# Four column tiles of 32 rows for eight of sixteen experts, and three experts fixed in advance, in a one-core inference step

## The chip, the core and the metric

The kernel runs on one core of a Trainium2 chip. The core has a matmul engine (TensorE, PE in the rows; PEld is its weight load), VectorE (DVE), ScalarE (ACT), GpSimd (POOL) and SyncE (SP), which here only issues DMAs. Sixteen DMA engines move data between the chip's memory (HBM), SBUF and DRAM scratch tensors. The metric is the device time of one execution in microseconds. Everything is fp32.

## The reference

One layer of a hybrid backbone on 128 context tokens and 256 latent tokens of width 1024. The part before the experts (norm, modulation, a state-space mixer, a gated MLP mixer, the output projection) is not touched by the change. The part that is:

```python
scores = sigmoid(h @ router_w); sel = scores + router_b          # 16 experts in 4 groups
g = argmax over groups of the sum of the group's top 2 of sel
expert = top 2 of sel within group g;  w = scores[expert] / sum
hg = h @ w_gate[e];  hu = h @ w_up[e]                            # 1024 -> 512
moe = sum over the two experts of w * ((silu(hg) * hu) @ w_down[e])   # 512 -> 1024
x = x + gate2 * moe;   y = rmsnorm(x, final_norm_w)
```

384 tokens choose two experts each: 768 pairs. With the inputs drawn by setup_inputs the experts 0 to 15 get 108, 37, 143, 90, 9, 41, 48, 32, 16, 18, 12, 4, 63, 52, 18 and 77 pairs. An expert's weights are 2 MiB of gate, 2 MiB of up and 2 MiB of down, so the sixteen are 96 MiB, and each is read once.

## The kernel before

**Stages.** Up to about 240 us of the span the mixers and the output projection run. Then the router picks the experts (240 to 258 us), and the tokens are sorted by expert: GpSimd scatters every token's row to a scratch tensor in HBM, `sorted_tokens` (`hsd`), at the place of its pair, and six tiles of 128 rows are read back (`hsr`, one `hs_in` semaphore each), transposed on TensorE (`sorted_columns`, L738) and copied by ACT and DVE into `hTs`. While that goes on, TensorE already works on the first expert, whose rows it picks by one-hot matmuls (L825, L832).

**Places.** The experts are worked on in sixteen places. Place 0 is expert 0 and place 1 expert 1, so that their weights load long before the router has run; the others are ordered on the chip by their number of pairs, by a key of ranks (`turn_key`). Pairs of one place lie side by side in `sorted_tokens`.

**Passes.** A pass takes 64 rows of one place. `gate_up` (L754) holds 64 rows as stationary operand in two column tiles and streams 512 columns (256 of gate and 256 of up) through each; 8 chunks of the contraction times 2 tiles is 16 matmuls. An fp32 matmul here leaves two records in the trace, so a pass shows 32. `down` (L767) is 8 matmuls, 16 records. Between them ACT takes silu of the gate half out of PSUM (`gate`, L1110), DVE multiplies (`multiply`, L1661), TensorE transposes the product (`transposes`, L777, 2 records) and DVE copies it back (`turn_over`, L1666). The order on TensorE is a pipeline: gate_up of the next pass, then down of the pass before, then the transposes of the next. ACT copies the result of down (`evacuate`, L1125) and sends it with two DMAs to `sorted_outputs` (L1129); before it sends, it waits until the pass before has landed. A place with more than 64 rows has a second pass, with more than 128 a third. What is left of the possible passes is made up for by adding to the semaphores (`skipped`), which count PASSES per place on every engine.

**Weights.** Three sets of buffers. Place p uses set p % 3, and SP loads it in `reload`: gate and up (four DMAs, L389) when all gate_up passes of place p-3 are done, down (one DMA, L394) when the last down of place p-3 is done, which on TensorE comes after the first gate_up of place p-2. SP's DMAs are in program order.

**The start.** The sets of places 0 and 1 load from 180 us on. Set 2 is known only after the router: its buffers overlap those of the sorted tiles, so SP loads the gate weights after `int_done` (the integers that the engines branch on) and the up and down weights after the last sorted tile is transposed (`hs_ready` 12, L430). Then comes place 3.

**The end.** The last three passes stay in SBUF; the other results are picked up by GpSimd from `sorted_outputs` (L1916), and TensorE adds all up (L863, L886). Then the final norm and the output.

The names that the change and the prediction touch: `load_gate_up`, `load_down`, `reload` (SP), `gate_up`, `down`, `transposes`, `skipped`, `second_pass`, `sorted_columns` (PE), `gate`, `evacuate`, `last_pass`, `sorted_copy` (ACT), `stage_x` (L1656, which copies the rows of a place into the stationary buffer `xs`), `turn_over`, `multiply`, `to_next` (DVE).

## Time and profile before

| what | us |
|---|---|
| median of three runs | 545.04 (544.37 to 546.21) |
| span of the profiled execution, first to last instruction | 544.1 |
| PE busy in the span | 480.4 (88%) |
| DVE, ACT, POOL busy | 236.0, 148.2, 104.4 |
| moved by DMA | 164.64 MB, mean 303 GB/s |

The profile gives the profiled execution as its span alone; what lies around it is in the runs' own times, whose median is 0.9 us above that span. Busy time of PE counts pipelined matmuls with modelled ends, so a busy PE is not one at its peak. The span in 40 slices of 13.6 us shows three parts: until slice 17 the mixers, slices 18 and 19 the router with no DMA at all, then from slice 22 on the experts, with PE at nine tenths or more and the DMA engines full at the same time, and at the end three slices in which the DMA is nearly empty. A DMA share slightly above 1 is a full one.

### The profile page before, as it was taken

What the parts mean: (1) busy time and instruction counts of PE and PEld (TensorE: products, weight loads), DVE (VectorE), ACT (ScalarE), POOL (GpSimd) and SP (SyncE); (2) the same over time, 40 slices, a digit from 0 to 9 for tenths busy, and PEclk for the clock granted to TensorE, in tenths of its full rate; (3) what the DMA queues carried; (4) which work ended last, traced back from release to release, by engine and by line L of the source; (5) the groups of instructions that cost most, each with busy time, mean ns of one, the idle gap of its engine ahead of it and who ended that gap; (6) DMA issues with size and microseconds to landing.
All of it is one profiled execution on the core that took longest, in us unless ns stands there. A gap on an engine that the chain in (4) does not pass through costs nothing. (4 is left out here: it accounts for less than half of the span.)

```text
span 544.1 us, 8978 instructions
## 1 busy us (share of the span) xinstructions
PE 480.4 (88%) x3278; PEld 233.3 (43%) x3279; DVE 236.0 (43%) x590; ACT 148.2 (27%) x289; POOL 104.4 (19%) x187
## 2 busy tenths in 40 slices
PE   2788979899969999995996999899998999999893
PEld 1135669655559644573344333333333333333331
DVE  2698994999963300867663101111011101111045
ACT  3645794532147610151102010110001100101142
POOL 3000250988870203500500000000000000000300
PEclk9988999999999999995998999999999999999998
DMA  8993046449497999220696999999999999999932
GB/s 278 339 400 112 1 154 217 166 166 363 143 391 269 369 366 417 82 86 1 239 385 243 410 423 418 418 418 416 421 421 419 419 417 419 417 420 421 403 120 116
DMA packets 42571, 164.64 MB, mean 303 GB/s; under 512 B 3314, under 2 KB 4106, under 8 KB 32676
## 3 DMA queue, kind: packets, MB, share of 16 engines
q1 hardware_dynamic: 35440, 144.22, 67.3%
q10 hardware_dynamic: 4580, 11.91, 5.8%
q0 software_dynamic: 2512, 7.99, 4.0%
q8 instruction: 24, 0.39, 0.3%
q14 instruction: 15, 0.12, 0.1%
HBM read 152.77 MB, written 11.34 MB: 302 GB/s over the span
## 5 line engine op out<-in xcount | busy, mean ns | idle before, releaser
L754 PE MATMUL psum<-arena 128*64 128x512 f32 x672 | 150.7, 601 | 16.7 <-DVE arena L1656 7.8
L754 PEld LDWEIGHTS psum<-arena 128*64 128x64 f32 x672 | 49.8, 138 | 103.7 <-issue 101.9
L767 PE MATMUL psum<-arena 128*64 128x512 f32 x336 | 75.9, 592 | 0.0
L1661 DVE TENSOR_TENSOR arena<-arena,psum 128x256 f32<-128x256 f32 x21 | 8.8, 421 | 143.4 <-ACT arena L1110 143.2
L1916 POOL DMA_INDIRECT arena<-sorted_outputs,src_u x6 | 5.7, 951 | 244.1 <-DMA sorted_outputs<-arena 242.6
L767 PEld LDWEIGHTS psum<-arena 128*64 128x64 f32 x336 | 25.7, 137 | 45.9 <-issue 45.9
L1110 ACT ACTIVATE arena<-psum 128x256 f32<-128x256 f32 x21 | 8.0, 383 | 130.0 <-PE psum L754 114.5
L664 PE MATMUL psum<-arena 128*128 128x512 f32 x96 | 42.2, 594 | 0.0
L1125 ACT ACTIVATE arena<-psum 128x512 f32<-128x512 f32 x19 | 11.3, 597 | 58.0 <-PE psum L767 58.0
L664 PEld LDWEIGHTS psum<-arena 128*128 128x128 f32 x96 | 17.9, 190 | 21.2 <-issue 20.9
L1656 DVE COPY arena<-arena 128x512 f32 x31 | 13.1, 423 | 30.4 <-issue 30.4
L487 PE MATMUL psum<-arena 128*2 128x512 f32 x64 | 18.4, 734 | 8.1 <-DMA arena<-in_w_mod 8.1
L528 PE MATMUL psum<-arena 128*128 128x388 f32 x64 | 23.8, 521 | 1.1 <-ACT arena L957 1.1
L940 ACT ACTIVATE arena<-arena 128x512 f32<-128x512 f32 x32 | 20.9, 715 | 7.7 <-DVE arena L1371 7.7
L536 PE MATMUL psum<-arena 128*128 128x388 f32 x64 | 21.1, 491 | 0.0
L617 PE MATMUL psum<-arena 128*128 128x512 f32 x48 | 20.9, 594 | 0.0
L1666 DVE COPY arena<-psum 128x256 f32<-128x256 f32 x21 | 8.9, 425 | 25.3 <-PEq L786 13.7
L1860 POOL TENSOR_TENSOR arena<-arena 128x64 f32<-128x64 f32 x32 | 14.8, 464 | 22.3 <-DVEq L1462 19.9
L472 PE MATMUL psum<-arena 128*2 128x128 f32 x512 | 15.4, 273 | 1.4 <-DMA arena<-in_w_mod 1.4
L528 PEld LDWEIGHTS psum<-arena 128*128 128x128 f32 x64 | 12.4, 203 | 9.0 <-issue 3.0
L1862 POOL TENSOR_TENSOR arena<-arena 128x64 f32<-128x64 f32 x32 | 15.2, 476 | 2.5
L536 PEld LDWEIGHTS psum<-arena 128*128 128x128 f32 x64 | 12.1, 190 | 8.4
(355 smaller groups left out, 657.3 us busy)
## 6 DMA issues: line engine op xcount, KB each, us to landing
arena<-in_w_gate SPq DMA_DIRECT2D x32, 1024.0 KB, 15.7
arena<-in_w_up SPq DMA_DIRECT2D x32, 1024.0 KB, 18.1
arena<-in_w_down SPq DMA_DIRECT2D x16, 2048.0 KB, 15.2
arena<-in_w_mod SPq DMA_DIRECT2D x12, 2048.0 KB, 13.0
arena<-in_w_in SPq DMA_DIRECT2D x3, 2048.0 KB, 19.2
sorted_outputs<-arena ACTq DMA_DIRECT2D x38, 128.0 KB, 6.3
arena<-in_w_out SPq DMA_DIRECT2D x2, 2048.0 KB, 16.7
arena<-modulation_rows ACTq DMA_DIRECT2D x4, 1024.0 KB, 10.7
```

Source lines behind the costliest of these rows:

```text
L472: last = mm(out[t], sil[:, k, :], w[:, k, t * P:t * P + P], start=(k == 0), stop=False)
L487: last = mm(bank[(4, 7)[c]][32 * t:32 * t + 2, :], sil[:, k, :], w[:, kk, t * D + c * 512:t * D + c * 512 + 512], start=(k == 0), stop=(k ...
L528: last = mm(bank[c][:, 0:TOK], w[:, k, c * P:(c + 1) * P], h1T[:, k, :], start=(k == 0), stop=(k == KD - 1))
L536: last = mm(out, w[:, k, c * P:(c + 1) * P], h1T[:, k, :], start=(k == 0), stop=(k == KD - 1))
L617: last = mm(bank[b][:, :], h1T[:, k, T0[t]:T0[t] + P], w[:, k, :], start=(k == 0), stop=(k == KD - 1))
L664: last = mm(bank[OUT_BANK[2 * t + h]][:, :], yT[:, k, T0[t]:T0[t] + P], wout[h][:, k, :], start=(k == 4), stop=(k == 3))
L754: last = mm(bank[0][HALF * t:HALF * t + HALF, :], xs[:, side, k, :], gu[:, :, k, t * 256:t * 256 + 256], start=(k == 0), stop=(k == KD - 1))
L767: last = mm(bank[4][HALF * h:HALF * h + HALF, :], hiddenT[:, s * P + t * HALF:s * P + t * HALF + HALF], dn[:, 2 * t + s, h * 512:h * 512 + ...
L940: last = A(out[:, :, 16 * g:16 * g + 16], made[i % 4], ACT.Copy, scale=side[:, c:c + 1])
L1656: cp(xs[:, side], hTs[:, :, bass.ds(row, HALF)]).then_inc(S("x_staged"), 1)
L1860: p(G.tensor_tensor(pt1, prev, Tre, ALU.mult))
L1862: w(G.tensor_tensor(nxt, nxt, pt1, ALU.add))
```

## The change

1. **Lots of 32.** Places 1, 2, 4, 5, 7, 8, 10 and 11 (`in_parts`) run in passes of 32 rows. `gate_up` then uses four column tiles of 32 stationary columns and streams 256 columns through each: 32 matmuls a pass, 64 records. `down` is 16 matmuls of 256 columns. There is one transpose in place of two, and ACT, DVE and the two DMAs of a result handle half as much. PASSES is 12 in place of 6; the loop over places handles its three places by name (one full, two in parts), and the last three places are written out.
2. **Three fixed experts.** Places 0, 1, 2 are the experts 0, 4 and 8 (EARLY), with 108, 9 and 16 pairs. The other thirteen are ordered by a new key. With the pairs above the places hold:

| place | 0 | 1 | 2 | 3 | 4 | 5 | 6 | 7 | 8 | 9 | 10 | 11 | 12 | 13 | 14 | 15 |
|---|---|---|---|---|---|---|---|---|---|---|---|---|---|---|---|---|
| pairs before | 108 | 37 | 90 | 63 | 52 | 48 | 41 | 143 | 32 | 18 | 77 | 18 | 16 | 12 | 9 | 4 |
| passes of 64 before | 2 | 1 | 2 | 1 | 1 | 1 | 1 | 3 | 1 | 1 | 2 | 1 | 1 | 1 | 1 | 1 |
| pairs now | 108 | 9 | 16 | 143 | 37 | 32 | 90 | 18 | 18 | 77 | 12 | 4 | 63 | 52 | 48 | 41 |
| passes of 64 now | 2 | - | - | 3 | - | - | 2 | - | - | 2 | - | - | 1 | 1 | 1 | 1 |
| passes of 32 now | - | 1 | 1 | - | 2 | 1 | - | 1 | 1 | - | 1 | 1 | - | - | - | - |

3. **Loads.** The buffers change places: the third set's gate and up lie where the output projection's weights were, and load when that projection's last matmul is done (`wo_ready` 6). The sorted tiles lie over the third set's down buffer (`h2`'s slot); tiles 0, 1, 2 and 4 load as before, tile 3 after `int_done`, and tile 5 takes tile 0's place, so ACT issues its load after tile 0 is transposed. SP issues the gate and up weights of place 3 when the second gate_up of place 0 is done, ahead of the wait for the sorted tiles; the down weights of place 2 after that wait, and those of place 3 after the last down of place 0. TensorE's code for place 0 is written out so that the semaphore `gated` is topped up right after the second gate_up.
4. Some small operations on DVE (the number of passes for lots of 32) ahead of `int_done`, and four on POOL (`in_parts`).

```diff
-PASSES = 6
+PASSES = 12
+FULL = 6
+PART = 32
+EARLY = (0, 4, 8)
-        hsr = view(slot(7), 6, D)
+        hsr = [view(at, D) for at in (slot(6), slot(6) + 1024, slot(6) + 2048, slot(6) + 3072, F + 12544, slot(6))]
-            b = (3, 0, 6)[j]
-            return view(slot(b), 2, KD, DE), view(slot(b + 2), 4, D)
+            gu, dn = ((3, 5), (0, 2), (7, 6))[j]
+            return view(slot(gu), 2, KD, DE), view(slot(dn), 4, D)
...
             sp.wait_ge(S("fin_done"), 1)
-            load_gate_up(0, 0)
-            load_down(0, 0)
+            load_gate_up(0, EARLY[0])
+            load_down(0, EARLY[0])
             sp.wait_ge(S("unit_used"), 15)
-            load_gate_up(1, 1)
+            load_gate_up(1, EARLY[1])
             sp.wait_ge(S("yt_done"), 4)
             sp.wait_ge(S("modd_in5"), 32)
-            load_down(1, 1)
+            load_down(1, EARLY[1])
+            sp.wait_ge(S("wo_ready"), 6)
+            load_gate_up(2, EARLY[2])
+            def load_sorted(t):
+                sp.dma_start(hsr[t], hsd[t * P:(t + 1) * P, :]).then_inc(S(f"hs_in{t}"), 16)
             sp.wait_ge(S("tok_sent"), 16 * 6)
-            for t in range(6):
-                sp.dma_start(hsr[:, t, :], hsd[t * P:(t + 1) * P, :]).then_inc(S(f"hs_in{t}"), 16)
-            sp.wait_ge(S("first_ready"), 1)
+            sp.wait_ge(S("pad_sent"), 48)
+            sp.wait_ge(S("first_ready"), 4)
+            for t in (0, 1, 2):
+                load_sorted(t)
+            load_sorted(4)
             sp.wait_ge(S("onehots_done"), 1)
-            sp.wait_ge(S("pad_sent"), 48)
             sp.wait_ge(S("int_done"), 1)
-            third = expert_at(2)
-            for k, sem in ((0, "gu_in2"), (KD // 2, "gu_rest2")):
-                sp.dma_start(expert_weights(2)[0][:, 0:1, k:k + KD // 2],
-                             wg[:, bass.ds(third, 1), k:k + KD // 2, :]).then_inc(S(sem), 16)
+            load_sorted(3)
+            fourth = expert_at(SETS)
+            sp.wait_ge(S("gated"), PASSES)
+            load_gate_up(0, fourth)
             sp.wait_ge(S("hs_ready"), 12)
...
-            def gate_up(j, at, fresh, side=0):
+            def gate_up(j, at, fresh, side=0, part=False):
+                rows, cols = (PART, P) if part else (HALF, 256)
...
                 for k in range(KD):
-                    for t in range(2):
-                        last = mm(bank[0][HALF * t:HALF * t + HALF, :], xs[:, side, k, :],
-                                  gu[:, :, k, t * 256:t * 256 + 256], start=(k == 0), stop=(k == KD - 1))
+                    for t in range(P // rows):
+                        last = mm(bank[0][rows * t:rows * t + rows, 0:2 * cols], xs[:, side, k, 0:rows],
+                                  gu[:, :, k, t * cols:t * cols + cols], start=(k == 0), stop=(k == KD - 1))
                 last.then_inc(S("gated"), 1)
-            def down(j, fresh, turned, evacuated):
+            def down(j, fresh, turned, evacuated, part=False):
-                for s in range(2):
-                    for t in range(2):
-                        for h in range(2):
-                            last = mm(bank[4][HALF * h:HALF * h + HALF, :],
-                                      hiddenT[:, s * P + t * HALF:s * P + t * HALF + HALF],
-                                      dn[:, 2 * t + s, h * 512:h * 512 + 512],
-                                      start=(s == 0 and t == 0), stop=(s == 1 and t == 1))
+                if part:
+                    for t in range(4):
+                        for h in range(4):
+                            last = mm(bank[4][PART * h:PART * h + PART, 0:256], hiddenT[:, t * PART:t * PART + PART],
+                                      dn[:, t, h * 256:h * 256 + 256], start=(t == 0), stop=(t == 3))
+                else:
+                    for s in range(2):
+                        for t in range(2):
+                            for h in range(2):
+                                last = mm(bank[4][HALF * h:HALF * h + HALF, :],
+                                          hiddenT[:, s * P + t * HALF:s * P + t * HALF + HALF],
+                                          dn[:, 2 * t + s, h * 512:h * 512 + 512],
+                                          start=(s == 0 and t == 0), stop=(s == 1 and t == 1))
                 last.then_inc(S("downed"), 1)
-            def transposes(at):
+            def transposes(at, part=False):
                 pe.wait_ge(S("multiplied"), at + 1)
-                for s in range(2):
+                for s in range(1 if part else 2):
...
+            def part_rest(j, e, use):
+                n = pe.value_load(n_i[0:1, bass.ds(e, 1)], min_val=0, max_val=NT * P)
+                def part_pass(at):
+                    gate_up(j, at, None, 0, True)
+                    down(j, use + 1, at, at + -1, True)
+                    transposes(at, True)
+                with pe.If(n > PART):
+                    gate_up(j, turn(1, e), None, 1, True)
+                    down(j, use + 1, turn(1, e), turn(0, e), True)
+                    transposes(turn(1, e), True)
+                    with pe.If(n > HALF):
+                        with pe.Fori(2, 6) as q:
+                            part_pass(q + turn(0, e))
...
-                later_passes(0, 0, 0, first_n)
+                gate_up(0, turn(1, 0), None, 1)
+                with pe.If(first_n > P):
...
+                with pe.Else():
+                    pe.wait_ge(S("gated"), turn(2, 0))
+                    pe.sem_inc(S("gated"), PASSES - 2)
+                    down(0, 1, turn(1, 0), turn(0, 0))
+                    transposes(turn(1, 0))
+                    pe.wait_ge(S("crossed"), turn(2, 0))
+                    pe.wait_ge(S("downed"), turn(2, 0))
+                    pe.sem_inc(S("crossed"), PASSES - 2)
+                    pe.sem_inc(S("downed"), PASSES - 2)
+                    sorted_tiles()
...
-                    expert_rest((j + 1) % SETS, e + 1, use)
+                    use, other = i + (j + 1) // SETS, (j + 1) % SETS
+                    gate_up(other, turn(0, e + 1), use + 1, 0, other > 0)
+                    down(j, i + 1, turn(PASSES, e), turn(PASSES - 1, e), j > 0)
+                    transposes(turn(0, e + 1), other > 0)
+                    if other > 0:
+                        part_rest(other, e + 1, use)
+                    else:
+                        expert_rest(other, e + 1, use)
+            for j in range(SETS):
...
-            def evacuate(y, downed, before, row):
+            def evacuate(y, downed, before, row, part=False):
                 act.wait_ge(S("downed"), downed + 1)
-                A(ystage[:, y, :], bank[4][:, :], ACT.Copy).then_inc(S("evacuated"), 1)
+                cols = 256 if part else 512
+                A(ystage[:, y, 0:cols], bank[4][:, 0:cols], ACT.Copy).then_inc(S("evacuated"), 1)
                 act.wait_ge(S("evacuated"), before + 2)
                 act.wait_ge(S("written"), before * 32 + 32)
                 for h in range(2):
-                    act.dma_start(ysd[bass.ds(row, HALF), h * 512:h * 512 + 512],
-                                  ystage[HALF * h:HALF * h + HALF, y, :]).then_inc(S("written"), 16)
+                    half = ystage[HALF * h:HALF * h + HALF, y, 0:cols]
+                    if part:
+                        dst = ysd[bass.ds(row, PART), h * 512:h * 512 + 512].rearrange("r (q c) -> q r c", q=2)
+                    else:
+                        dst = ysd[bass.ds(row, HALF), h * 512:h * 512 + 512]
+                    act.dma_start(dst, half).then_inc(S("written"), 16)
...
-            for t in range(6):
+                second_pass(0, 2)
+            sorted_copy(0)
+            act.wait_ge(S("hs_ready"), 2)
+            act.dma_start(hsr[5], hsd[5 * P:6 * P, :]).then_inc(S("hs_in5"), 16)
+            for t in range(1, 6):
...
+            rank, turn_key, counted_rank = r1[:, 0, :], key, r2[:, 0, :]
             v(V_.tensor_reduce(rank, larger, AX.X, ALU.add))
-            v(ts(turn_key, rank, 0.15, None, ALU.mult))
-            for r in (2.0, 4.0):
-                v(stt(turn_key, rank, r, turn_key, ALU.is_equal, ALU.add))
+            v(ts(counted_rank, rank, 0.5, 1.75, ALU.mult, ALU.add))
+            v(stt(counted_rank, rank, 9.5, counted_rank, ALU.is_lt, ALU.mult))
+            v(stt(turn_key, rank, 0.5, counted_rank, ALU.mult, ALU.add))
```

DVE has the same three changes as ACT: a `part` argument that halves the columns of `multiply` and `turn_over` and the rows of `stage_x`, a `part_rest`, and the loop over three places.

SP's instructions from the load of place 1's down weights to the gate weights of place 3 (sorted_tokens are the sorted tiles, 128x2048 a half of a gate or up matrix), before:

```order
L394 DMA arena<-in_w_down 128x4x1024 [waits modd_in5,yt_done]
L419 DMA arena<-sorted_tokens 128x1024 [waits tok_sent]
L419 DMA arena<-sorted_tokens 128x1024 x5
L398 TENSOR_LOAD exp_i [waits pad_sent,int_done,onehots_done,first_ready]
L398 ISA x2
L426 ISA
L426 DMA arena<-in_w_gate 128x2048
L426 ISA
L426 DMA arena<-in_w_gate 128x2048
L430 DMA arena<-in_w_up 128x2048 [waits hs_ready]
L430 DMA arena<-in_w_up 128x2048
L394 DMA arena<-in_w_down 128x4x1024
```

and now:

```order
L393 DMA arena<-in_w_gate 128x2048 [waits wo_ready]
L393 DMA arena<-in_w_up 128x2048
L393 DMA arena<-in_w_gate 128x2048
L393 DMA arena<-in_w_up 128x2048
L425 DMA arena<-sorted_tokens 128x1024 [waits first_ready,pad_sent,tok_sent]
L425 DMA arena<-sorted_tokens 128x1024 x3
L425 DMA arena<-sorted_tokens 128x1024 [waits int_done,onehots_done]
L402 TENSOR_LOAD exp_i
L402 ISA x2
L393 ISA [waits gated]
L393 DMA arena<-in_w_gate 128x2048
L393 DMA arena<-in_w_up 128x2048
```

The four loads of place 2 have moved ahead of the sorted tiles, one sorted tile is gone from the queue and another has a wait of its own, and the loads of place 3 now wait for TensorE's gate_up alone. Behind them stand the two loads of down weights, of place 2 and of place 3, and then the loads of place 4:

```order
L398 DMA arena<-in_w_down 128x4x1024 [waits hs_ready]
L398 DMA arena<-in_w_down 128x4x1024 [waits downed]
L402 TENSOR_LOAD exp_i
L402 ISA x2
L393 ISA [waits gated]
```

Before, only `hs_ready` stood between the sorted tiles and the loads of places 2 and 3, now a load of down weights stands on each of two waits.

ACT's queue at the sorted tiles (L1129 or L1218 sends place 0's first result, L1114 or L1197 copies a sorted tile out of PSUM), before:

```order
L1129 DMA sorted_outputs<-arena 64x512
L1129 ISA
L1129 DMA sorted_outputs<-arena 64x512
L1175 UNCONDITIONAL_BRANCH
L1114 ACTIVATE arena<-psum 128x4x128 [waits hs_ready] x6
```

and now:

```order
L1218 DMA sorted_outputs<-arena 64x512
L1218 ISA
L1218 DMA sorted_outputs<-arena 64x512
L1288 UNCONDITIONAL_BRANCH
L1197 ACTIVATE arena<-psum 128x4x128 [waits hs_ready]
L1292 DMA arena<-sorted_tokens 128x1024 [waits hs_ready]
L1197 ACTIVATE arena<-psum 128x4x128 [waits hs_ready] x5
```

The load of tile 5 stands behind the two result DMAs and the copy of tile 0, and TensorE's last eight transposes wait for it.

## Rows read from the trace of the kernel before

**Rows 1.** DMA between 300 and 480 us: packets and rate, queues, landing times.

```profile
DMA packets 14932, 75.34 MB, mean 419 GB/s; under 512 B 1385, under 2 KB 1385, under 8 KB 9137
q1 hardware_dynamic: 12525, 71.31, 96.0%
sorted_outputs<-arena ACTq DMA_DIRECT2D x32, 128.0 KB, 6.4
```

**Rows 2.** Stretches: PE, PEld, DVE, ACT, POOL busy us, PE clock, DMA share, GB/s.

```profile
236.00:260.00 24.00, 17.69 (x87) 12.00 (x87) 17.08 (x62) 8.25 (x15) 1.06 (x1) 0.64 0.00 1
...
288.00:292.00 4.00, 1.96 (x18) 1.77 (x16) 2.08 (x4) 1.55 (x3) 0.00 (x0) 1.00 0.28 55
292.00:296.00 4.00, 2.42 (x8) 0.77 (x10) 1.09 (x3) 0.00 (x0) 0.00 (x0) 0.73 1.00 403
296.00:300.00 4.00, 4.00 (x18) 1.33 (x16) 0.00 (x0) 0.00 (x0) 0.00 (x0) 0.84 0.98 395
```

**Rows 3.** Timeline of PE: start, duration, instructions [idle before, releaser]; places 0 to 2.

```profile
272.71 7.09 PE L754 MATMUL psum<-arena 128*64 128x512 f32 x32 [0.67 <-issue]
279.62 3.61 PE L767 MATMUL psum<-arena 128*64 128x512 f32 x16
...
286.15 3.81 PE L738 MATMUL psum<-arena 128*128 128x128 f32 x32 [0.77 <-ACT arena L1114]
293.58 8.78 PE L754 MATMUL psum<-arena 128*64 128x512 f32 x32 [3.62 <-DVE arena L1656]
302.19 3.61 PE L767 MATMUL psum<-arena 128*64 128x512 f32 x16
305.73 0.44 PE L777 MATMUL psum<-arena 128*128 128x128 f32 x2
306.88 7.09 PE L754 MATMUL psum<-arena 128*64 128x512 f32 x32 [0.72 <-PEq L786]
...
317.70 7.09 PE L754 MATMUL psum<-arena 128*64 128x512 f32 x32
```

**Rows 4.** Timeline of PE, the place with three passes and the next.

```profile
376.49 7.09 PE L754 MATMUL psum<-arena 128*64 128x512 f32 x32 [1.03 <-DVE arena L1656]
...
409.91 7.09 PE L754 MATMUL psum<-arena 128*64 128x512 f32 x32 [0.89 <-PEq L786]
...
421.49 7.09 PE L754 MATMUL psum<-arena 128*64 128x512 f32 x32 [0.69 <-PEq L786]
```

**Rows 5.** Timeline of PE where four column tiles are used.

```profile
80.45 1.93 PE L472 MATMUL psum<-arena 128*2 128x128 f32 x64
82.20 0.40 PE L476 MATMUL psum<-arena 128*2 128x128 f32 x8
...
93.43 0.87 PE L581 MATMUL psum<-arena 128*32 128x96 f32 x32
94.11 0.48 PE L587 MATMUL psum<-arena 128*32 128x32 f32 x32
```

**Rows 6.** Timeline of SP, the waiting loads.

```profile
289.99 0.81 SPq L430 DMA_DIRECT2D arena<-in_w_up  x2
...
305.83 0.39 SPq L394 DMA_DIRECT2D arena<-in_w_down  x1
...
409.24 0.33 SPq L389 DMA_DIRECT2D arena<-in_w_gate  x1
```

**Rows 7.** Timelines: DVE and ACT at place 0, DVE at place 1.

```profile
271.12 0.42 DVE L1661 TENSOR_TENSOR arena<-arena,psum 128x256 f32<-128x256 f32 x1 [2.07 <-ACT arena L1110]
...
284.04 1.32 ACTq L1129 DMA_DIRECT2D sorted_outputs<-arena  x2
...
305.35 0.43 DVE L1656 COPY arena<-arena 128x512 f32 x1 [2.11 <-issue]
```

**Rows 8.** DMAs that write or read sorted_tokens, shortest, median and longest.

```profile
DMA to landing us min/median/max: 3.2/5.1/8.4
```

**Rows 9.** Timeline of PE at the last place.

```profile
507.10 3.65 PE L754 MATMUL psum<-arena 128*64 128x512 f32 x16 [0.83 <-DMA arena<-in_w_up]
```

More of the change, by code:

```diff
@@ L216, in build @@
         fin = small(2, Q)
+        in_parts = small(NE)
         epsc = small(1)
@@ L850, in _ @@
             with pe.Else():
                 skipped(0, 1)
-            with pe.Fori(0, 5) as i:
+                sorted_tiles()
+            with pe.Fori(0, 4) as i:
                 for j in range(SETS):
                     e = i * SETS + j
-                    use = i + (j + 1) // SETS
-                    gate_up((j + 1) % SETS, turn(0, e + 1), use + 1)
-                    down(j, i + 1, turn(PASSES, e), turn(PASSES - 1, e))
-                    transposes(turn(0, e + 1))
-                    expert_rest((j + 1) % SETS, e + 1, use)
+                    use, other = i + (j + 1) // SETS, (j + 1) % SETS
[6 more added lines that the diff above has]
+                        expert_rest(other, e + 1, use)
@@ L861, in late_part @@
+            for j in range(SETS):
+                e = 4 * SETS + j
+                use, other = 4 + (j + 1) // SETS, (j + 1) % SETS
+                gate_up(other, turn(0, e + 1), use + 1)
+                down(j, 5, turn(PASSES, e), turn(PASSES - 1, e))
+                transposes(turn(0, e + 1))
+                expert_rest(other, e + 1, use)
             def late_part(part, t, h):
@@ L1105, in _, with gate @@
                       S("first_staged"), 1)
-            def gate(at):
+            def gate(at, part=False):
+                cols = P if part else 256
                 act.wait_ge(S("gated"), at + 1)
-                A(sg[:, :], bank[0][:, 0:256], ACT.Silu).then_inc(S("silued"), 1)
+                A(sg[:, 0:cols], bank[0][:, 0:cols], ACT.Silu).then_inc(S("silued"), 1)
             def sorted_copy(t):
@@ L1776, in _ @@
                 skipped(0, 1)
-            with dve.Fori(0, NE - 1) as e:
+            with dve.Fori(0, 4) as i:
+                for j in range(SETS):
+                    e, other = i * SETS + j, (j + 1) % SETS
+                    to_next(e, j > 0, other > 0)
+                    if other > 0:
+                        part_rest(e + 1)
+                    else:
+                        expert_rest(e + 1)
+            with dve.Fori(4 * SETS, NE - 1) as e:
                 to_next(e)
```

192 lines of the change are left out of this document (140 added, 52 removed).

## The prediction, made before the changed kernel was run

> **What bounds the kernel now.** I read the strip of 40 slices first, then stretches of a few us, then the timelines of PE and SP. From slice 22 on two resources are full together. The DMA engines move 419 GB/s without a gap from 300 to 480 us, 71.3 MB of it weights on SP's queue [rows 1]. PE starts a new place 11.6 to 11.8 us after the last and a further pass of the same place 10.8 us after the pass before: 306.88 to 317.70 in place 2, and 33.4 for the three passes from 376.49 to 409.91 [rows 3, 4]. Twenty passes from 293.58 on end at the last gate_up. Which of the two ends last is seen at the last place: the second half of its gate_up starts at 507.10 and was released by the DMA of up weights, after only 0.83 us of waiting [rows 9]. So both arrive together. After it comes a tail of down, adding up and the final norm that the change leaves alone: 544.1 - 507.1 = 37 us. The question is when the last gate and up weights land, T, now 507.
>
> The weight stream starts at 290.9: SP issued at 289.99 and the stretch 288 to 292 has a DMA share of 0.28, 1.1 us of 4 [rows 2, 6]. Before that lies a hole: from 236 to 260 the DMA is all but empty [rows 2].
>
> **PE's part of the change.** Now 13 passes are of 64 rows and 9 of 32. Four column tiles already run in this kernel: 64 records of 128 columns take 82.20 - 80.45 = 1.75 us, 27.3 ns each, and 32 records with 32 stationary columns and 96 streamed take 0.68 us, 21 ns each [rows 5]. Two tiles of 512 columns take 279.62 - 272.71 = 6.91 us for 32 records, 216 ns each [rows 3]. By columns 128 at 27.3 is 256 at 54.6, so gate_up of 32 rows is 64 x 54.6 = 3.5 us in place of 6.9, and down 32 x 54.6 = 1.75 in place of 3.54 (305.73 - 302.19). The row of 21 ns says that loading 32 columns ahead of each record fits under that. What follows a gate_up before the next place's rows are staged doesn't shrink: from the end of place 1's gate_up (302.19) to the end of DVE's copy (305.78) 3.6 us [rows 3, 7]. A place in one part thus takes 3.5 + 3.7 = 7.2 us, or 8.2 behind a full down, against 11.7. Summed by places 3 to 14: 33.4 + 14.5 + 7.2 + 22.6 + 8.2 + 7.2 + 22.6 + 8.2 + 7.2 + 3 x 11.7 = 166 us, while twelve places of weights take 12 x 6.29 MB / 0.40 = 189. PE falls out of the bound; the stream sets the end.
>
> **What the stream saves.** From its start to T it carries 80 MiB of weights before (up of place 2, its down, twelve places, gate and up of the last). Now gate and up of place 2 load at 237, in the hole, and gate and up of place 3 when the second gate_up of place 0 ends, at 279.8, when DMA has only sorted tiles left. 72 MiB stay: 8.4 MB less. The results written shrink as well, 64 KB a DMA for a part: 18 passes x 0.262 = 4.7 MB before, 10 x 0.262 + 9 x 0.131 = 3.8 MB now. Together 9.3 MB / 419 = 22.2 us less.
>
> **What it pays: a later start.** The down weights of place 2 wait for the last sorted tile, those of place 3 for the last down of place 0, and behind the latter waits everything else on SP's queue, in program order. Tile 5 is loaded only after tile 0 is transposed, on ACT's queue behind the two result DMAs, which end at 285.36 [rows 7]. With 0.6 for ACT's copy of tile 0 and 0.3 for TensorE's new wait on its own semaphore ahead of down, the issue is at 286.3. The landing is not in the trace. Bounds: 3.2 and 8.4, the ends of the row of DMAs of that tensor [rows 8]; the nearest row is a result DMA of ACT behind the weight stream, 6.4 [rows 1]. I take 6.5: 292.8. Its eight transposes take 3.81 / 4 = 0.95, so 293.8 against 289.96. From there to place 1's gate_up 3.6 as before: 297.4 against 293.58.
>
> That gate_up follows idle time. Before, after 3.6 idle us, the clock was 0.73 in 292 to 296 and 0.84 in 296 to 300, part of it at 1.2 GHz, and gate_up took 8.78 for 7.09, 1.7 lost [rows 2, 3]. Now PE idles longer, in two pieces, and the clock is likely at 1.2 GHz from the first record; I take 2.0 lost (bounds 0 and 3.5): end at 302.9. Down of place 0 ends 3.54 later, 306.4; SP issues 0.1 later (305.83 against 305.73) and data flow 0.9 after that: 307.4, where the stream before started at 290.9. Cost 16.5 us.
>
> **A stall at place 3.** Place 3 now holds 143 pairs, three full passes. Place 2's gate_up starts 4.7 after place 1's ended (302.19 to 306.88): 307.6, takes 3.5, and place 3's starts 3.7 later, 314.8. Gate and up of place 6 wait for all of place 3's passes: before, the three-pass place started at 376.49 and SP issued at 409.24, 32.75 later [rows 4, 6]. So 347.5, data at 348.4. Until then the queue holds down 3, gate, up and down of 4 and of 5: 14 MiB and 1.05 MB of results, 15.7 MB / 419 = 37.5 us from 307.4, which is 344.9. The stream stands still for 3.5 us. At place 6 (two passes, SP's issue 21.9 after its start) the same sum gives 393 against a queue that lasts to 396, and at place 9 still more room: no stall.
>
> Sum: -22.2 + 16.5 + 3.5 = -2.2 us. The last gate_up starts after idle time too, up to 1.7 lost, most of it under the wait between its halves: +0.2. The small DVE operations (six of 0.2 us ahead of `int_done`) add up to 1.2 and are hidden under gate_up of place 0, for which DVE idles 2.07 us before its product [rows 7]. The sum is made on the span of 544.1; the runs' median is 0.9 above it, and I carry the difference of -2.0 over: **543.0 us**.
>
> **Two rules from the skill.** The row has ACT's DMAs of 128 KB land in 6.4 us behind a full SP queue [rows 1]. The Trainium skill (DMA: Bandwidth & Descriptors, Queues, rings and completion order) says that each DMA engine takes the queues in turn, packet by packet. By that tile 5, four times as large, would share with place 3's weights and land in some 6.4 + 0.39 MB / 210 = 8.3 us, for a sum of -0.4 instead of -2.2; only part of it counts, as those weights end near 291.
>
> PE lost 1.7 us after 3.6 idle us [rows 2, 3]. The Trainium skill (TensorE: Matmul & The Clock Gate, HAM oscillation) warns that a kernel which waits for DMA between bursts of matmuls goes back to half clock at each of them. That speaks against making PE the engine that waits, and is rival 3.
>
> **Rivals.**
> 1. *The start is less late.* Tile 5 lands in 3.2 us, because place 3's weights are nearly through: place 1 starts at 294.1, with a clock loss as before. -2.0 - 3.3 - 0.3: 539.4. For it: only some 1.5 MB of those weights are left when it is issued (4.2 MB from 280.6 at 419). Against: the 6.4 us of the same queue. The same time follows if place 3's stall doesn't come (-3.5).
> 2. *The start is later still (slower).* Tile 5 lands after 8.4 (+1.9), and the clock stays at 1.2 GHz through all of place 1's part gate_up and into down of place 0 (+1.5, and +1 in down): the stream starts near 312. +2.4 on the median, and with the clock loss at the end 548. It decides from a start of the stream later than 309.4, which eats the whole gain.
> 3. *The clock at the end.* PE waits at places 12 to 15 about 4 us each. If it is at 1.2 GHz there, places 12 to 14 hide it under the DMA, but the last gate_up loses 3.4: 546.4. Against: its halves land 5 us apart, so the first half hides what it loses.
> 4. *Four tiles don't overlap better than two.* A part then costs a full pass, PE has 22 passes, and places 3 and 6 stall the stream by 8 and 10 us: 560. Against: the 27.3 ns of rows 5.
>
> **Chances.** Forecast 0.38 (its own range 541 to 545), rival 1 0.27, rival 2 0.20, rival 3 0.08, rival 4 0.05, anything else 0.02. A difference under 0.3% (1.6 us, 543.4 to 546.7) can't be told from none here. Faster: rival 1 and 0.6 of the forecast, 0.50. Same: the rest of the forecast, half of rival 3 and a little of rival 2, 0.25. Slower: 0.25. The range leaves out rival 4 and the outer halves of rivals 1 and 2: 538 to 548.5.
>
> **What would show it.** Right: a part gate_up of 64 records in 3.5 us; gate and up of place 2 landing before 250; SP's down of place 3 issued at 306.5 and place 6's gate weights at 347.5 with a hole of 3 to 4 us before them; from place 12 on PE waiting for DMA; the last half gate_up at 505. Wrong in size: place 1's gate_up starting before 295 or after 300, since every us of it moves T by one. Wrong in kind: PE waiting for no DMA after place 9, or records of parts over 80 ns apart.

## The result and the profile after

The changed kernel took 628.05 us (median of four runs, 621.89 to 633.45) and the kernel before, beside it, 545.62 (544.37 to 546.48). The ratio is 1.1415 (95% interval 1.1361 to 1.1468). Forecast were 543.0 (538 to 548.5). Its runs lie in pairs, 622 and 623 and twice 633; the ratio and all comparisons below use the lower pair, 622.4, and the trace is of an upper run.

The page of the kernel after: header, busy time, 40 slices, queues.

```profile
span 631.0 us, 9919 instructions
...
PE 481.0 (76%) x3751; PEld 242.3 (38%) x3752; DVE 234.5 (37%) x600; ACT 146.4 (23%) x291; POOL 105.4 (17%) x190
...
PE   2869899998999996986756959827795346966694
...
PEclk9989899999999996789667988969898587888988
...
GB/s 302 365 306 0 134 186 149 179 360 205 386 282 407 361 100 267 163 210 311 137 378 379 219 184 240 417 286 211 269 418 419 340 185 365 398 416 120 247 6 100
...
q8 instruction: 45, 0.74, 0.5%
q14 instruction: 34, 0.28, 0.1%
```

PE's busy time is what it was (481.0 against 480.4 us), though it has less to do: part of it runs at a lower clock. A slice is 15.8 us here. From the nineteenth on (284 us) neither PE nor DMA stays full, where before the DMA moved 419 GB/s without a gap [rows 1]. The last two rows are the ones to notice: the queues that carry instructions. The page of before has 24 packets on q8 and 15 on q14. From 340 us to the last places (to 500 before, to 550 after) it has three in all, the changed kernel 31.

The timeline of PE after (start, duration, instructions, idle before and its releaser):

```profile
302.36 2.77 PE L765 MATMUL psum<-arena 128*32 128x256 f32 x21 [3.49 <-DVE arena L1780]
...
322.90 5.55 PE L765 MATMUL psum<-arena 128*32 128x256 f32 x50 [4.23 <-issue]
...
336.26 9.80 PE L765 MATMUL psum<-arena 128*64 128x512 f32 x32 [5.60 <-PEq L804]
...
369.50 0.44 PE L794 MATMUL psum<-arena 128*128 128x128 f32 x2
377.63 6.16 PE L765 MATMUL psum<-arena 128*32 128x256 f32 x64 [7.69 <-issue]
...
387.56 3.66 PE L765 MATMUL psum<-arena 128*32 128x256 f32 x64
391.04 1.91 PE L778 MATMUL psum<-arena 128*32 128x256 f32 x32
...
401.64 7.09 PE L765 MATMUL psum<-arena 128*64 128x512 f32 x32 [1.15 <-DVE arena L1780]
421.21 3.64 PE L778 MATMUL psum<-arena 128*32 128x256 f32 x32 [12.49 <-ACTq L1224]
...
584.05 7.09 PE L765 MATMUL psum<-arena 128*64 128x512 f32 x32 [1.48 <-PEq L804]
```

Two kinds of gap stand here that [rows 3, 4] don't have. One says "issue" or PEq: PE waits for nothing that a semaphore shows, and it can fall into the middle of a gate_up (322.90). The other waits for ACT. Undisturbed passes are as short as forecast: 64 records in 3.66 us, down in 1.91. ACT's timeline at the 12.49:

```profile
393.01 0.38 ACT L1209 ACTIVATE arena<-psum 128x256 f32<-128x256 f32 x1 [1.45 <-PE psum L778]
395.79 1.77 ACTq L1218 DMA_DIRECT2D sorted_outputs<-arena  x2
...
400.29 0.39 ACT L1209 ACTIVATE arena<-psum 128x256 f32<-128x256 f32 x1 [1.45 <-PE psum L778]
417.62 1.73 ACTq L1218 DMA_DIRECT2D sorted_outputs<-arena  x2
420.50 0.20 ACT L1260 ACTIVATE arena<-arena 128x1 f32<-128x1 f32 x1 [19.82 <-DMA sorted_outputs<-arena]
421.32 0.39 ACT L1193 ACTIVATE arena<-psum 128x256 f32<-128x256 f32 x1 [0.62 <-ACTq L1224]
```

The copy at 400.29 is done at 400.68, but its DMAs go out at 417.62, since the result before (sent 395.79 to 397.56) has not landed until then: 20 us, where a result took 6.4 before [rows 1]. Behind them waits the next silu.

### The profile page after: what moved, and what is told of

Read it like the earlier page. It is cut to its first block and busy times, and to the rows that moved or that the text cites. A ratio compares the mean times of both kernels' runs of the same rounds, so it can differ in the third digit from the quotient of the medians.

```text
span 631.0 us, 9919 instructions
## 1 busy us (share of the span) xinstructions
PE 481.0 (76%) x3751; PEld 242.3 (38%) x3752; DVE 234.5 (37%) x600; ACT 146.4 (23%) x291; POOL 105.4 (17%) x190
## 5 line engine op out<-in xcount | busy, mean ns | idle before, releaser
L765 PE MATMUL psum<-arena 128*32 128x256 f32 (+1 forms) x992 | 153.0, 564 | 67.4 <-issue 32.6
L765 PEld LDWEIGHTS psum<-arena 128*32 128x32 f32 (+1 forms) x992 | 56.1, 144 | 152.7 <-issue 145.6
L784 PE MATMUL psum<-arena 128*64 128x512 f32 x208 | 50.2, 626 | 5.4 <-issue 5.0
L784 PEld LDWEIGHTS psum<-arena 128*64 128x64 f32 x208 | 15.8, 143 | 36.8 <-issue 36.8
L778 PE MATMUL psum<-arena 128*32 128x256 f32 x288 | 19.9, 409 | 13.0 <-ACTq L1224 13.0
L674 PEld LDWEIGHTS psum<-arena 128*128 128x128 f32 x96 | 17.9, 190 | 21.2 <-issue 20.9
L1780 DVE COPY arena<-arena 128x256 f32 (+1 forms) x31 | 11.0, 354 | 29.2 <-issue 15.8
L1209 ACT ACTIVATE arena<-psum 128x512 f32<-128x512 f32 (+1 forms) x20 | 10.0, 501 | 44.4 <-PE psum L784 29.0
L778 PEld LDWEIGHTS psum<-arena 128*32 128x32 f32 x288 | 9.9, 117 | 23.3 <-issue 18.4
L2025 POOL TENSOR_TENSOR arena<-arena 128x64 f32<-128x64 f32 x32 | 14.9, 464 | 23.0 <-DVEq L1585 20.6
```

Of the source, the lines that this page charges most:

```text
L674: last = mm(bank[OUT_BANK[2 * t + h]][:, :], yT[:, k, T0[t]:T0[t] + P], wout[h][:, k, :], start=(k == 4), stop=(k == 3))
L765: last = mm(bank[0][rows * t:rows * t + rows, 0:2 * cols], xs[:, side, k, 0:rows], gu[:, :, k, t * cols:t * cols + cols], start=(k == 0), ...
L778: last = mm(bank[4][PART * h:PART * h + PART, 0:256], hiddenT[:, t * PART:t * PART + PART], dn[:, t, h * 256:h * 256 + 256], start=(t == 0 ...
L784: last = mm(bank[4][HALF * h:HALF * h + HALF, :], hiddenT[:, s * P + t * HALF:s * P + t * HALF + HALF], dn[:, 2 * t + s, h * 512:h * 512 + ...
L1780: cp(xs[:, side, :, 0:rows], hTs[:, :, bass.ds(row, rows)]).then_inc(S("x_staged"), 1)
L2025: p(G.tensor_tensor(pt1, prev, Tre, ALU.mult))
```

## The experiments

Theory F: the longer loop bodies of the engines no longer stay on them, and after jumps each waits for instructions that come by DMA behind the weights. Theory R: a part's result lands late. Rivals: the new order of places and loads, the part passes, the clock. The clock was not varied by itself in any run. Its mean over a run is 0.89 in the changed kernel, 0.94 in the fastest version of it, and 0.95 to 0.97 in the kernel before, so it doesn't order the times by itself. How much of a stall's cost is the clock's was not taken apart.

**Size of the code.** In the first run PE's, in the second ACT's and DVE's, in the third all code for a third and later part pass is left out. No part place has over 64 rows, so the work done is unchanged.

```diff
                     transposes(turn(1, e), True)
-                    with pe.If(n > HALF):
-                        ... (Fori over part passes 2 to 5, and 6 to 11)
-                    with pe.Else():
-                        skipped(e, 2)
+                    skipped(e, 2)
```

> The changed kernel, with TensorE's code for a third and later part pass of a 32-row place left out (never reached with these inputs; the executed work is the same). TensorE's loop body falls from 626 rows of the built program, 496 of them matmuls, to 388 with 300 (before: 427 with 312). Theory F (the loop bodies no longer stay on the engine, so that jumps wait for instructions that come by DMA behind the weights): the instruction packets on q8 fall from 45 to about 30, the idle stretches of 4 to 8 us behind L804 and inside gate_up go, and the time falls from 622 to 565-590, the rest being ACT's and DVE's code. Rival O (order of the places and loads, part passes themselves): 622, unchanged within 3.

Measured 596.06 (593.35 to 603.43), ratio 1.0877 to before; q8 30 packets, as F said; the time is 6 us over F's range. PE's code carries 27 us.

> The changed kernel, with ACT's and DVE's code for a third and later part pass left out (never reached with these inputs), TensorE's kept. ACT's loop body falls from 359 rows to 173 (before 182), DVE's from 261 to 133 (before 67). Theory F: the packets on q14 fall from 34 to about 17, the ACT gaps of 10 to 20 us go, time 595-612. Rival O: 622. A form of F in which TensorE's fetches alone count: 618-622.

Measured 615 and 620, and 633 and 635; q14 16 packets. Some 5 us at most (622.4 less 617.4), where F gave 10 or more. Perhaps these engines mostly fetch while they wait for PE anyway; no run shows it.

> The changed kernel, with the code for a third and later part pass left out on TensorE, ACT and DVE (never reached with these inputs). Theory F: q8 about 30 packets, q14 about 17, no idle stretch of TensorE over 2.5 us after 320 other than for data, time 538-552, which is what was predicted of the change. Rival O: 622; a mix of both: 560-600.

Measured 590.67 (586.18 to 593.14), ratio 1.0777. F alone gave 538-552, so it is right in kind and too small: it holds 32 of the 77 us. The other 45 are of another cause. ACT's timeline in this run:

```profile
379.64 1.76 ACTq L1209 DMA_DIRECT2D sorted_outputs<-arena  x2
381.95 0.28 ACT L1184 ACTIVATE arena<-psum 128x128 f32<-128x128 f32 x1 [5.15 <-ACTq L1216]
383.69 0.38 ACT L1200 ACTIVATE arena<-psum 128x256 f32<-128x256 f32 x1 [1.46 <-PE psum L778]
400.77 1.72 ACTq L1209 DMA_DIRECT2D sorted_outputs<-arena  x2
```

From 379 to 401 the instruction queues are empty and the DMA moves 423 GB/s, yet 400.77 - 381.40 = 19.4 us pass before the result has landed.

**The kernel before with a longer body.** The never reached branch for over 160 rows is written out with extra matmuls.

```diff
-                        with pe.Fori(3, PASSES) as q:
-                            gate_up(j, q + turn(0, e), None)
+                        for q in range(3, PASSES):
+                            for _ in range(3):
+                                gate_up(j, turn(q, e), None)
```

> The kernel before, with TensorE's never reached branch for more than 160 rows made longer (its three passes written out, each with its gate_up matmuls three times): loop body of 871 rows with 756 matmuls in place of 427 with 312. No 32-row part, old order, old loads; the work executed is that of before. Theory F: q8 goes from 24 packets to 40 or more, gaps of 4 to 8 us appear between the places, time 580-630. Rival O: 545, unchanged within 2.

Measured 577.39 (575.65 to 579.35), ratio 1.0574 (1.0517 to 1.0631); q8 34 packets. Skipped code alone, with nothing of the change's work, costs 31 us. That is a little less than F gave (580-630, 40 packets or more).

**How a part's result is sent.**

```diff
-                for h in range(2):
-                    half = ystage[HALF * h:HALF * h + HALF, y, 0:cols]
-                    dst = ysd[bass.ds(row, PART), h * 512:h * 512 + 512].rearrange("r (q c) -> q r c", q=2)
+                for h in range(4):
+                    act.dma_start(ysd[bass.ds(row, PART), h * 256:h * 256 + 256],
+                                  ystage[PART * h:PART * h + PART, y, 0:256]).then_inc(S("written"), 16)
```

> The short-code kernel of the run before (no code for a third part pass), and the result of a part pass sent with four DMAs of 32 rows by 256 columns in place of two whose target has an outermost dimension of two; the same bytes go to the same places. In that kernel ACT waited 10 to 20 us several times for the result before to land. Theory R (a part's result takes about 20 us to land behind the weight stream, because a transfer with an outermost dimension of two runs on two of the sixteen DMA engines; ACT waits for it before it sends the next, and the silu behind that wait comes late): landing 5 to 8 us, ACT's waits for sorted_outputs below 10 us in sum, time 540-553. Rival S (results are late because ACT itself stalls, or because the shorter passes ask for more of them than can land): 575-592, waits of 10 us and over stay.

Measured 548.83 (545.51 to 554.63, ten runs), ratio 1.0022 (0.9991 to 1.0052), no difference from before. ACT no longer waits for `sorted_outputs`. What PE waits for in this run (us in total, times, longest), and the page's row of the full results with their median to landing:

```profile
PE psum L765 <- DMA arena<-in_w_up: 22.7, 7, 5.3
...
PE psum L748 <- DMA arena<-sorted_tokens: 4.9, 1, 4.9
```

```profile
sorted_outputs<-arena ACTq DMA_DIRECT2D x22, 128.0 KB, 6.7
```

A part's DMA, now of 32 KB, lands in a median of 5.4 us between 340 and 500 us. PE now waits for weights: this is the bound that was forecast. Time, landing and waits are as R said.

> The changed kernel with all its code, and a part's result sent with four DMAs of 32 rows. ACT's loop body grows from 359 rows to 461. If the two causes add (about 35 us of code, 40 us of results): 575-590. If the late results are a consequence of the instruction fetches: 605-622. If the fetches hurt only in the shadow of the late results: 545-560.

Measured in two pairs, 586 and 588, 627 and 634; what parts them by 43 us is not known. The means of the lower times are 622.4 (long code) and 590.2 (short) with two DMAs, and 587.0 and 547.5 with four. So the four DMAs are worth 35 us with the long code and 43 with the short, and the short code 40 with them and 32 without. By these times the two causes about add.

> The kernel before, with the result of each place's last pass (64 rows by 512 columns, twice) sent by the same two DMAs, but with the target written as an outermost dimension of two times 32 rows: the same bytes and addresses, no 32-row pass, short code. Theory R: these DMAs land in 15 to 25 us in place of 6.3, ACT waits for them after nearly every pass, time 590-720. Rival S: the addresses are the same, so nothing changes, 545.

Measured 546.43 (545.42 to 552.61), unchanged, but it tests nothing: in the built program the two times 32 neighbouring rows are one dimension of 64 again, `[[1024, 64], [1, 512]]` (stride and size of each dimension, in elements), and the page shows the same 4,580 packets on ACT's queue q10 as before. A part's result in the changed kernel has `[[256, 2], [1024, 32], [1, 256]]`. So once more, with rows that can't be merged (`"(r q) c -> q r c"`, built as `[[1024, 2], [2048, 32], [1, 512]]`):

> The kernel before; each place's last result (sixteen of them) is sent by the same two DMAs of 64 rows, with a target whose outermost dimension is two and can't be merged (row 2r+q for partition 32q+r): the output rows stand in another order, bytes and sizes are the same. In the run with a target of two times 32 neighbouring rows the compiled DMA had one dimension of 64 again. Theory R (two of sixteen engines, 15 to 25 us to land): TensorE waits after most passes, time 580-700. Rival S: 545, unchanged.

Measured 637.25 (633.98 to 648.91), ratio 1.1569 (1.1503 to 1.1636). ACT's timeline and its wait in sum:

```profile
415.83 1.72 ACTq L1132 DMA_DIRECT2D sorted_outputs<-arena  x2
...
423.57 0.60 ACT L1125 ACTIVATE arena<-psum 128x512 f32<-128x512 f32 x1 [3.05 <-PE psum L767]
440.62 1.71 ACTq L1132 DMA_DIRECT2D sorted_outputs<-arena  x2
```

```profile
ACT arena L1164 <- DMA sorted_outputs<-arena: 136.3, 12, 19.3
```

With the same bytes and passes, a result takes 440.62 - 417.55 = 23 us to land. This probe puts the rows in another order, so its output is not that of the layer, and it has its rows 8 KB apart in place of 4 as well. In the changed kernel the rows of a part's target stay 4 KB apart and it is late too, and with an outermost dimension of 32 the same part lands in 5.4 us. What the late ones have in common is the outermost two, so R's effect is shown. The Trainium skill (DMA: Bandwidth & Descriptors, Rules for kernel authors) says it outright: an outermost dimension of size c below 16 confines the whole DMA to at most c engines. By that each of two engines gets 32 rows of a DMA, and each of sixteen gets 4 of a plain one. The runs show the time; the engine count itself is the page's.

**Order and loads without parts.** All passes 64 rows (`part` false throughout, `in_parts` zero).

> The changed kernel with its order of places, its three fixed experts and its loads, but every pass 64 rows as before (no column tiles of 32; TensorE's loop body 442 rows with 312 matmuls, ACT's 281, DVE's 209). If loads and order cost nothing beside the start, as forecast: TensorE is the bound again, 21 full passes from 302 on: 552-562. Rival O (order and loads carry a part of the loss): over 570. Less than 546: the early loads alone would gain.

Measured 570.13 (569.89 to 572.49), just over the line, so order and loads do carry a loss without parts. PE sets the pace up to place 14, so each loss on it is paid in full: place 1 starts at 299.06 against 293.58 [rows 3], place 3 has a gap of 4.84 at L804 in the first iteration, and the gate_up behind it takes 9.58 for 7.09. That is 13 of the 22 us. The others stand at the end: the last place's gate_up waits 5.81 us for up weights and its first half takes 5.89 for 3.65, and the first matmul of the final sum waits 4.27 where it was 0.83 before. So here the weights come last after all. The parts without their two mistakes win back 21 us over this (548.83), by taking PE out of the bound.

**The start.** Forecast was tile 5's landing at 292.8. PE waited for it until 297.08 in the changed kernel, until 296.87 in the short-code one with four DMAs, and until 293.4 to 294.6 in the five other runs with this order on TensorE, in each 8.5 to 8.7 us from its issue. Tiles 0 to 4 are transposed ahead of down of place 0:

```diff
                     pe.sem_inc(S("gated"), PASSES - 2)
+                    for t in range(5):
+                        sorted_columns(t)
                     down(0, 1, turn(1, 0), turn(0, 0))
                     transposes(turn(1, 0))
-                    sorted_tiles()
+                    sorted_columns(5)
```

> The short-code kernel with four result DMAs, and on TensorE tiles 0 to 4 transposed ahead of down of place 0's second pass (ACT copies them ahead of its result), so that the 4.9 us in which TensorE waited for tile 5 hold that down. If the kernel is now bound by the weight stream and so by its start, as forecast: place 1's first gate_up starts about 297.5 in place of 302.3, and the time falls by 4 to 6 us, to 541-545 (0.5 to 1% below before). Rival: the stream after 330 is full anyway and the start is made up for: 546-549.

Measured 542.69 (541.34 to 544.58) against 548.45, ratio 0.9884 (0.9833 to 0.9935), a small difference whose interval leaves out 1. It is the only version faster than before, and it leaves out the paths for over 64 rows in a part place. Its timeline of PE:

```profile
286.78 3.65 PE L784 MATMUL psum<-arena 128*64 128x512 f32 x16
...
292.03 1.16 PE L748 MATMUL psum<-arena 128*128 128x128 f32 x8 [1.23 <-DMA arena<-sorted_tokens]
296.68 5.35 PE L765 MATMUL psum<-arena 128*32 128x256 f32 x64 [3.48 <-DVE arena L1769]
...
313.31 7.09 PE L765 MATMUL psum<-arena 128*64 128x512 f32 x32 [1.14 <-DVE arena L1769]
...
448.91 9.51 PE L765 MATMUL psum<-arena 128*64 128x512 f32 x32 [6.70 <-DMA arena<-in_w_up]
...
504.49 3.65 PE L765 MATMUL psum<-arena 128*64 128x512 f32 x16 [1.11 <-DMA arena<-in_w_up]
```

**What decides the price of code.** All with the kernel before; the branch for over 160 rows is made longer on one or two engines.

```diff
-                        for q in range(3, PASSES):
+                        for q in 10 * [*range(3, PASSES)]:      # ACT; on DVE 26, 23 or 20 times
```

> The kernel before with ACT's and DVE's never reached branch for more than 160 rows made longer (ACT's loop body 506 rows in place of 182, DVE's 292 in place of 67), TensorE's as before. Theory F for these engines, with the 3 to 5 us that leaving such code out gave: q14 goes from 15 packets to 25 or more, time 548-556. Rival: they fetch while they wait for other engines and nothing shows, 545.

695.18 (694.29 to 701.26), ratio 1.2693; q14 127 packets. Far over both theories.

> The kernel before, ACT's loop body alone longer (506 rows in place of 182, two places each iteration); DVE's and TensorE's short. Both together had cost 147 us, and nearly all idle time of TensorE stood behind DVE's copy of the next rows (12 us at each place). If DVE's body of 292 rows for one place did that: here 548-575. If ACT did: over 620.

580.84 (580.50 to 581.14), ratio 1.0649; q14 53. Between the two, nearer to the first.

> The kernel before, DVE's loop body alone longer (292 rows in place of 67, one place each iteration); ACT's and TensorE's short. If DVE waits at each of 15 places for its code: 640-690, with gaps of about 12 us ahead of the copy of the next rows. If ACT was the cause: 545-560.

696.64 (693.57 to 698.88), ratio 1.2755; q14 90. DVE alone costs what both did. Its timeline at three places, against a 2.11 before the same copy in [rows 7]:

```profile
351.94 0.43 DVE L1656 COPY arena<-arena 128x512 f32 x1 [6.86 <-issue]
...
373.85 0.43 DVE L1656 COPY arena<-arena 128x512 f32 x1 [12.01 <-issue]
...
397.11 0.43 DVE L1656 COPY arena<-arena 128x512 f32 x1 [12.37 <-issue]
```

> The kernel before with DVE's loop body of 238 rows (before 67; 292 rows cost 151 us and took q14 from 15 packets to 90). Step theory (the body stops to fit between 238 and 292): 545-549, q14 about 20. Rival G (each skipped row costs): three quarters of the 151 us, about 655.

555.71 (555.27 to 556.19), ratio 1.0162 (1.0110 to 1.0214); q14 19. G is out; the step theory is 7 us too low.

> As the run before, DVE's body 265 rows, as in the changed kernel (261, though there for three places). Step theory with the step at 256: 620-700, q14 over 60. Step theory with the step higher: 545-549. Rival G: about 675.

554.78 (553.95 to 557.81), ratio 1.0158; q14 18. The cost jumps between 265 and 292 rows on DVE. Below that two places are slow and then none. DVE's timeline at 238 rows:

```profile
297.23 0.43 DVE L1656 COPY arena<-arena 128x512 f32 x1 [7.45 <-issue]
...
315.80 0.43 DVE L1656 COPY arena<-arena 128x512 f32 x1 [7.61 <-issue]
...
338.51 0.43 DVE L1656 COPY arena<-arena 128x512 f32 x1 [1.74 <-issue]
...
350.82 0.43 DVE L1656 COPY arena<-arena 128x512 f32 x1 [2.27 <-issue]
```

> The kernel before, TensorE's never reached loop for more than 160 rows with its gate_up matmuls four times in place of once: loop body 571 rows of the built program, 456 of them matmuls. Two records per matmul and a weight load to each make four hardware instructions of one matmul, so the body is about 1,940 (before 1,363; the changed kernel 2,114; the longer one tried 3,139). Theory F with a size at which the body stops to fit, between 1,363 and 2,114: if that size is 2,048, this fits, 545-548 and q8 24 or 25 packets. Rival G (the cost grows with every row skipped, without a step): a third of the longer one's 31 us, 553-560.

636.95 (634.62 to 644.41), ratio 1.1669; q8 63. PE's timeline:

```profile
360.14 9.24 PE L754 MATMUL psum<-arena 128*64 128x512 f32 x32 [10.66 <-issue]
...
391.89 8.73 PE L754 MATMUL psum<-arena 128*64 128x512 f32 x32 [5.42 <-PEq L787]
...
416.31 8.47 PE L754 MATMUL psum<-arena 128*64 128x512 f32 x32 [11.88 <-issue]
```

> As the run before, with the gate_up matmuls five times: body 619 rows with 504 matmuls, about 2,130 hardware instructions, as the changed kernel's (626, 496, 2,114). Theory F with a step at 2,048: refetches in each of the five iterations, 560-580, q8 30 packets or more. Rival G: 556-562, 4 us over the run before. Rival H (the step lies above 2,130, and in the changed kernel the jumps themselves cost, not the size): 545-548.

639.86 (636.89 to 642.62), ratio 1.1715; q8 65.

> The kernel before with TensorE's body of 475 rows, 360 of them matmuls, about 1,550 hardware instructions (before 1,363; 1,940 cost 91 us and 39 packets on q8 more). Step theory: if the step lies above 1,555, 545-548 and q8 24 to 26. Rival G: a third of the 91 us, 575.

555.04 (551.91 to 557.58), ratio 1.0132 (1.0071 to 1.0193); q8 25. On PE the cost jumps between 1,555 and 1,940 of the instructions counted in the expectations; G falls with both steps. So there are two prices. The three runs under the step cost 9 to 10 us, paid at the first two places: on DVE in the rows above, on PE with place 1 at 298.49 for 293.58 and place 2 at 314.93 for 306.88, and no further loss after place 3. Over the step, waits come back in later iterations.

One thing was changed along with the length in all of these runs: place 0 has the same branch ahead of the loop, so the body also began at another point of the code. Length and place weren't told apart, so the two steps are those of this kernel.

The Trainium skill (Runtime: NRT & Kernel Launch, Instruction fetch mechanics) says that instructions come in blocks of 256 by prefetch in sequence, that crossing a block is mostly hidden, and that a taken branch out of the two-page window stalls for a DMA. By "mostly hidden" the change was free; by the branch rule it was not, and the gaps of 4 to 12 us are in line with the branch rule. While they last the DMA engines carry weights: ahead of PE's instruction at 360.14 the DMA share is 0.88 to 1.10 from 351 us on, ahead of DVE's at 397.11 it is 0.92 to 1.06 from 389 us on.

Left open: the run with PE's body of 3,139 cost less (31 us, ten packets) than those of 1,940 and 2,130 (91 and 94, about forty). Its extra code is jumped over in longer pieces, so that fewer blocks may be touched, but that wasn't tried. So the length of a body tells when to be wary. Packets of the instruction queues in every iteration show that it happened, but not its price: 38 more on ACT cost 35 us, 39 more on PE 91, 75 more on DVE 151, and one more on PE 9.

## Why the prediction was wrong

*The step that failed* is the one on PE's part, "What follows a gate_up before the next place's rows are staged doesn't shrink" and "A place in one part thus takes 3.5 + 3.7 = 7.2 us", summed to 166 us for places 3 to 14, "PE falls out of the bound; the stream sets the end". In the changed kernel these places take 584.05 - 336.26 = 248 us, and place 3 starts at 336.26 where the forecast had 314.8. It took for granted that nothing new stands between passes. Two new things did: the wait of ACT for a result that lands in 20 us (35 to 43 us of the loss), and the fetch of instructions (32 to 40 us). Results were counted by their bytes, "64 KB a DMA for a part", and not by the shape of their target nor by who waits behind them. Code was not counted at all, though the change to three places an iteration and twelve passes is what the order of instructions shows first. None of the four rivals held either cause.

*Passes.* Forecast 3.5 and 1.75 us, measured 3.66 and 1.91 to 1.93. Rival 4 falls.

*The stream.* With both causes gone it is the bound, as forecast: PE waits for up weights from about 438 us on (the 448.91 above), and the last half gate_up starts at 504.49, forecast 505. In the changed kernel the bytes saved bought nothing: from 340 to 550 us the DMA moved 307 GB/s, since SP's loads wait for passes that came late.

*The start.* This term was mis-sized. Tile 5 landed 8.5 us after its issue, forecast 6.5 with 8.4 as the upper bound; the prediction's other estimate, by queues that take turns, gave 8.3. In the changed kernel it was also issued late, at 288.5 for 286.3, since the second gate_up of place 0 began late and took 8.57 us for 7.09; in five other runs the issue came at 284.8 to 286.1. So place 1 began at 302.36 instead of 297.4, in those five at 298.8 to 300.0. Its gate_up, with a gap of 0.85 in it, ended 8.9 us later, where 3.5 and a loss of 2.0 were taken. The stream started with SP's down of place 3 at 314.87, forecast 306.5. This is rival 2 and some 4 us more. In the faster version, which puts down of place 0 into the wait, place 1 starts at 296.68, its gate_up takes 5.35 for 3.66, a loss of 1.7, and SP's down of place 3 goes out at about 305.7.

*The stall at place 3.* The forecast had gate weights of place 6 issued 32.7 us after place 3's start. In the faster version it is 344.49 - 313.31 = 31.2. The hole of 3.5 us before them didn't come: from 344 to 348 us the DMA share stays at 0.78 or more.

*A slip.* From 293.58 on the trace of before has nineteen passes, not twenty; no term of the sum uses the number.

So 543.0 was the time of the idea and not of the kernel. 542.69 was measured, but only after three things were mended that the forecast hadn't seen or had mis-sized. The two numbers agree partly by luck: beside that run the kernel before took 548.45, a gain of 5.8 us where 2.0 was forecast.

## What to carry to other kernels

Before an edit that adds branches or unrolled passes inside a loop, count the instructions of the loop's body on each engine and look at the instruction queues in the profile: packets that appear in every iteration are a warning, and gaps of several us called "issue" or PEq behind a branch are where the price is paid. Look at the built target of every DMA, however small it is, above all where the next one waits for it: an outermost dimension of two cost 35 us and more here, while 32 and 64 did not. Where a change makes a step shorter, ask of each wait hidden under the old length whether it still fits under the new one.

## What the hardware showed beyond that

A never executed branch of some 225 more rows on DVE, an engine that is idle most of the time, made the kernel 27% slower (546 to 697 us), because its short copy at the head of each place stands on the path. On ACT, 324 more rows cost 6.5%. The same 64 rows of 2 KB land in 6.3 us or in 23, by the order in which the target names them. And a stall can cost more than its row says: 64-row gate_ups behind gaps of 3.0 to 11.9 us took 8.4 to 10.1 us in place of 7.09, except for a few behind the shorter gaps. Behind the 10.66 us at 360.14 in PE's longer body the granted clock was 0.50 for the next 4 us, its lower level of 1.2 GHz.
